# Handing the second quarter of a transposed residual to TensorE in two pairs of slices, with the third quarter's transposes between them

## The reference

```
def rmsnorm(x, g):
    return x * lax.rsqrt(mean(x * x, -1) + EPS) * g

def swiglu(x, w_gate, w_up, w_down):
    return (silu(x @ w_gate) * (x @ w_up)) @ w_down

for l in range(2):
    x = x + 0.5 * swiglu(rmsnorm(x, ffn1_norm[l]), ffn1_w_gate[l], ffn1_w_up[l], ffn1_w_down[l])
    h = rmsnorm(x, mix_norm[l])
    ...                                    # projections h @ w_in, attention, gated linear attention
    x = x + y @ w_out[l]
    x = x + 0.5 * swiglu(rmsnorm(x, ffn2_norm[l]), ffn2_w_gate[l], ffn2_w_up[l], ffn2_w_down[l])
return rmsnorm(x, final_norm)
```

## Time and profile before

| | |
|---|---|
| time, median of 3 runs | 2364.39 us (2362.51 to 2365.77) |
| profiled execution, its own time | 2362.39 us |
| span of the profile (first to last instruction) | 2360.7 us |
| TensorE (PE) busy | 2318.9 us, 98% |
| VectorE (DVE) busy | 1586.1 us, 67% |
| ScalarE (ACT) busy | 1139.8 us, 48% |
| granted TensorE clock, mean | 0.996 |

### The profile page before, as it was taken

How to read it: one execution, slowest core, us unless ns; L and a number is a source line. 1 busy time by engine, 2 the same in 40 slices (tenths; PEclk the granted TensorE clock), 3 DMA queues, 4 the chain that set the end, 5 groups by cost and what they waited for, 6 DMA issues and landing times.

```text
span 2360.7 us, 32903 instructions
## 1 busy us (share of the span) xinstructions
PE 2318.9 (98%) x13270; PEld 1954.5 (83%) x13270; DVE 1586.1 (67%) x2396; ACT 1139.8 (48%) x1668; POOL 24.9 (1%) x65
## 2 busy tenths in 40 slices
PE   6999999999999999999999999999999999999998
PEld 4887887888889887888888988888888888888887
DVE  4677434657575777667776679676676676776766
ACT  4222223446433255445445478554464446875444
POOL 0001000010000000000000000000000000000000
PEclk8999999999999999999999999999999999999999
DMA  7468322433522234655555643445545555434553
GB/s 306 179 233 323 140 90 94 148 116 143 195 90 72 72 108 171 228 191 178 181 194 192 233 160 143 161 178 184 191 179 196 184 203 214 148 144 173 189 196 125
DMA packets 59311, 403.75 MB, mean 171 GB/s; under 512 B 8269, under 2 KB 8677, under 8 KB 11672
## 3 DMA queue, kind: packets, MB, share of 16 engines
q1 hardware_dynamic: 52992, 384.33, 44.9%
q10 hardware_dynamic: 3840, 9.43, 1.1%
q0 software_dynamic: 2336, 7.96, 1.1%
HBM read 400.60 MB, written 2.67 MB: 171 GB/s over the span
## 4 chain that ended last, share of the span: by engine, by line
PE 93%; DVE 3%; DMA 2%; ACT 1%; issue 1%; SPq 0%; ACTq 0%; DVEq 0%
PE pair L527 88%; DMA ring<-in_stream 2%; PE pair L937 1%; PE pair L1083 1%; PE pair L886 1%; DVE ring_parts L2389 0%; DVE ring_parts L2379 0%; PE pair L625 0%; ACT xT L1566 0%; PE pair L1352 0%; PE pair L1367 0%; PE pair L925 0%; DVE rows L2511 0%; PE pair L1337 0%; DVE X L2517 0%
## 5 line engine op out<-in xcount | busy, mean ns | idle before, releaser
L527 PE MATMUL pair<-xT_parts,ring_high 128*128 128x512 f32 x2112 | 747.4, 395 | 3.8 <-DVE xT_parts L2294 1.2
L527 PE MATMUL pair<-xT_parts,ring_parts 128*128 128x256 f32 (+2 forms) x2448 | 693.1, 298 | 3.3 <-DVE xT_parts L2307 1.4
L2379 DVE TENSOR_TENSOR ring_parts<-ring,ring_high 128x2048 fp32r<-128x2048 f32 x194 | 444.1, 2292 | 137.8 <-ACT ring_high L1623 137.7
L527 PEld LDWEIGHTS pair<-xT_parts,ring_parts 128*128 128x128 f32 (+1 forms) x2448 | 460.4, 188 | 44.3 <-issue 8.7
L527 PEld LDWEIGHTS pair<-xT_parts,ring_high 128*128 128x128 f32 x2112 | 384.5, 188 | 81.2 <-issue 2.0
L1623 ACT ACTIVATE ring_high<-ring 128x2048 fp32r<-128x2048 f32 x197 | 375.5, 1910 | 68.1 <-DMA ring<-in_stream 68.0
L2389 DVE TENSOR_TENSOR ring_parts<-ring,mix_high 128x1024 fp32r<-128x1024 f32 x144 | 169.2, 1218 | 38.1 <-ACT mix_high L1636 38.1
L1674 ACT ACTIVATE arena<-pair 128x512 f32<-128x512 f32 x110 | 65.9, 599 | 260.1 <-PE pair L527 260.1
L1636 ACT ACTIVATE mix_high<-ring 128x1024 fp32r<-128x1024 f32 x144 | 143.4, 1048 | 92.3 <-DMA ring<-in_stream 89.0
L527 PE MATMUL pair<-ring_parts,xT_parts 128*128 128x512 f32 (+1 forms) x448 | 173.9, 388 | 0.6 <-DVE ring_parts L2389 0.6
L527 PE MATMUL pair<-ring_parts,g_high 128*128 128x512 f32 x440 | 172.2, 391 | 0.2 <-issue 0.2
(11 more groups left out here) (439 smaller groups left out, 3867.6 us busy)
## 6 DMA issues: line engine op xcount, KB each, us to landing
ring<-in_stream SPq DMA_DIRECT2D x338, 1024.0 KB, 4.8
xn<-in_mods SPq DMA_DIRECT2D x14, 1024.0 KB, 4.9
arena<-in_mods SPq DMA_DIRECT2D x14, 1024.0 KB, 4.9
gateB<-gate_rows POOLq DMA_DIRECT2D x4, 512.0 KB, 7.6
xn<-maximum_rows POOLq DMA_DIRECT2D x8, 256.0 KB, 3.6
arena<-in_bT ACTq DMA_DIRECT2D x1, 1536.0 KB, 9.5
bias_scratch<-bias_row POOLq DMA_DIRECT2D x1, 1536.0 KB, 8.7
X<-in_x ACTq DMA_DIRECT2D x1, 1024.0 KB, 11.9
```

The source lines that it names most:

```text
L527: m = pe.matmul(o, l, r, start=start, stop=stop)
L2379: dve.tensor_tensor(out=ring_r[:, slot].rearrange("p a b -> p (a b)"), in0=w, in1=high[:, slot, :], op=ALU.subtract).then_inc(low_ready, 1)
```

## The change

The second quarter (q = 1) goes over in two pairs of slices. ACT raises `x_whole` after its second slice too, DVE splits k = 0, 1 and k = 2, 3 in two steps (`split_raw(1, 0, 2)` ahead of `update(0, 1)`, `split_raw(1, 2, 4)` behind it, ahead of `first_vars`), so that `x_split` counts five steps at a boundary. TensorE begins the next stage after the first pair: up tile 0's part 0 is made for k = 0, 1, then turn 2 comes, then k = 2, 3, then turn 3. Turn 2 leaves the end of the stage before. In the mixer's `pre_group` features 0 and 1 are made together for k = 0, 1, then turn 2, then their k = 2, 3, then turn 3, then features 2 and 3. At the `double` boundary the row of roots moves from behind up tile 1 to a place inside up tile 2, after three slices of its first half. The order of `update(1, 1)`, `split_raw(2)` and `low_part(0)` on DVE stays.

```diff
 def raw_start():
-    c.split += 4
+    c.split += 5
     c.raw += 1
     for part in range(2):
         for f in range(2):
-            if f == 0:
-                pe.wait_ge(x_split, c.split - 2 + 2 * part)
+            if part and f == 0:
+                pe.wait_ge(x_split, c.split)
             if part == 0 and f:
                 pe.wait_ge(low_half, c.raw)
             else:
                 low_wait(f)
-            up_steps(f, f, [(half, range(CW * part, CW * part + CW)) for half in range(2)])
+            if part or f:
+                up_steps(f, f, [(half, range(CW * part, CW * part + CW)) for half in range(2)])
+            else:
+                for first in (0, 2):
+                    pe.wait_ge(x_split, c.split - 3 + first // 2)
+                    up_steps(f, f, [(half, range(first, first + 2)) for half in range(2)])
+                    if first == 0:
+                        turn_raw(raw[0], 2, raw[1])
             if part:
                 owed.append(read[(c.chunk + f) % SLOTS])
-                if f == int(double):
+                if f == 0 and not double:
                     root_row()
             elif f == 0:
                 turn_raw(raw[0], 3, raw[1])
...
+                    elif f == 2 and double:
+                        up_steps(j, f, [(0, range(3))])
+                        root_row()
+                        steps = [(0, range(3, KD)), (1, range(KD))]
...
-                        if raw_next and f == FT - 1 and (n, t_) != (0, 0):
+                        if raw_next and f == FT - 1 and (n, t_) in ((0, 1), (1, 0)):
                             turn_raw("down", 2 * n + t_ - 1, c.resid)
...
-                        if raw_next and part_ and i:
+                        if raw_next and part_ and i in (1, 2):
                             turn_raw("quad", i - 1, c.acc)
...
                 for part in range(2):
-                    if turned is not None:
+                    by_pair = 2 if first and part == 0 else 0
+                    if turned is not None and not by_pair:
                         pe.wait_ge(x_split, turned - (0 if part else 2 if span == S else CW))
-                    for b, at in fs:
...
-                        if first and part == 0 and b is fs[0][0]:
-                            first()
+                    for q in range(by_pair):
+                        pe.wait_ge(x_split, turned - 3 + q)
+                        for b, at in fs[0:2]:
+                            feature(b, at, range(2 * q, 2 * q + 2))
+                        first(2 + q)
+                    for b, at in fs[by_pair:]:
+                        feature(b, at, range(CW * part, CW * part + CW))
...
-                c.split += 4
+                c.split += 5
...
-                pre_group(range(4), turned=c.split, between=mix_root_row, first=lambda: turn_raw("down", 3, at))
+                pre_group(range(4), turned=c.split, between=mix_root_row, first=lambda q: turn_raw("down", q, at))
...
-                    ins.then_inc(x_whole, 1)
+                        if j == 3 or j == 1 and q == 1:
+                            ins.then_inc(x_whole, 1)
...
-                def split_raw(q):
+                def split_raw(q, first=0, end=4):
                     h, t_ = divmod(q, 2)
-                    ks, at = slice(4 * h, 4 * h + 4), S + t_ * P
+                    ks, at = slice(4 * h + first, 4 * h + end), S + t_ * P
...
                 split_raw(0)
+                split_raw(1, 0, 2)
                 update(0, 1)
+                split_raw(1, 2, 4)
                 first_vars(2)
-                split_raw(1)
                 update(1, 1)
                 split_raw(2)
                 low_part(0)
```

More of the change, by code:

```diff
@@ L1185, in pre_group, with feature @@
                 ts = [(pre_bank(), slice(t_ * P, (t_ + 1) * P)) for t_ in tokens]
+                def feature(b, at, ks):
+                    for k in ks:
+                        wl, wh = mix_weights(k, slice(at, at + rows), True, 1 if beside is None else 2)
+                        mm(b[0:rows, 0:span], wl, whole[:, k, 0:span], k == 0, False)
+                        mm(b[0:rows, 0:span], wh, rest[:, k, 0:span], False, False)
+                        mm(b[0:rows, 0:span], wh, whole[:, k, 0:span], False, k == KD - 1,
+                           pre_full if k == KD - 1 else None)
                 for part in range(2):
-                    if turned is not None:
+                    by_pair = 2 if first and part == 0 else 0
+                    if turned is not None and not by_pair:
                         pe.wait_ge(x_split, turned - (0 if part else 2 if span == S else CW))
-                    for b, at in fs:
[L1190 to L1195, removed]
-                        if first and part == 0 and b is fs[0][0]:
-                            first()
+                    for q in range(by_pair):
[5 more added lines that the diff above has]
+                        feature(b, at, range(CW * part, CW * part + CW))
                     for b, ts_ in ts:
```

## The result

The changed kernel takes 2372.61 us (median of 6 runs, 2371.21 to 2377.95), the kernel before 2364.39, so the medians differ by 8.2 us. The prediction was 2372.1 and the sum behind it 7.75.

A forecast was written before the change was run, and what follows sets the result against it. PE was taken as busy 98% of the span, with the chain at the quad running from turn 2 to up tile 1. Terms 2.92 + 1.43 + 2.9 + 0.5 = 7.75 us on 2364.4 gave 2372.1, range 2367.0 to 2379.0.

The forecast's parts named there:

- The way: From turn 2 to up tile 1, 4.15 us; at both quad boundaries up tile 1 comes 1.46 later, together +2.92.
- FFN down: Down boundary into layer 1's FFN: up tile 0 starts 0.91 us earlier, up tile 1 1.43 later.
- Mixers: Two mixer boundaries: start 0.91 us earlier, row of roots 0.25 later at each, +0.5 together.
- Double: Double boundary: up tile 2 0.55 us later, ACT's take of the row of roots 3.2, first down tile 2.9.
- the slack of 0.33: Double boundary: DVE's `low` was expected to end about 0.33 us before PE needs it for the first down tile.
- (a): Rival: the clock falls behind the five new waits, 1.56 us each, 7.8 in all, giving 2379.9; chance 0.12.
- the prediction's own signs of being wrong: Up tile 1 2.2 us behind turn 2, granted clock below 1.00 behind a wait, or first down tile without a wait.
- (b): Rival: not slower, the way from turn 2 to up tile 1 is hidden behind PE's 2.16 us, giving 2362.1; chance 0.15.
- (c): Rival: the later row of roots at the double boundary costs nothing, sum 5.4 us, giving 2369.8; chance 0.10.
- (d): Rival: no early hand-over of the first pair, three starts lose the 0.91 us, sum 10.5, giving 2374.9; chance 0.05.

The follow-up runs named there:

- The first experiment: The changed kernel with low_part(0) put ahead of split_raw(2) on DVE: 2364.76 us, ratio 1.0007 to the kernel before.
- the row of roots alone: The kernel before with only the double boundary's row of roots moved into up tile 2: 2368.42 us beside 2362.91, ratio 1.0019.

## Why the prediction was right

That the medians differ by 8.2 where 7.75 was forecast is closer than the runs can tell. What bears the account is that the terms come out one by one in the table of distances above.

**The way.** "Turn 2 1.46 later, and nothing on DVE was moved past quarter 2's split" was the step that decides. The way stayed 4.15 at the quads, and the segments lost 1.48 and 1.4 for 1.46. The new wait is 1.7 and not 2.0, since a wait is counted from turn 3's modelled end, 0.60 behind its start, and I had taken 0.35; the time is the same. The first experiment turned the two instructions round, and the loss went.

**FFN down.** Up tile 0 follows the first copy after 3.38 (1737.72 in the profile after to 1741.10) in place of 4.21, 0.83 earlier for 0.91; up tile 1 after 9.02 in place of 7.48, +1.54 for +1.43.

**Mixers.** 0.90 earlier for 0.91 at the start; the row of roots 10.94 behind the first copy (1302.53 after) in place of 10.65, +0.29 for +0.25, with the wait of 0.60 that was to be seen. The segments say 0.4; where the last tenth lies stays open.

**Double.** Against the copy of quarter 1, at 1111.39 after and 1111.28 before: up tile 2 +0.56 for 0.55, ACT's take of the row +3.28 for 3.2, the first down tile +2.97 for 2.9 (1136.75 - 1111.39 less 1133.67 - 1111.28). The 0.31 between the last two is the slack of 0.33. The segment lost 0.3 more than the tile; that is the one term a little too small.

**The rivals.** (a), the clock, came once in ten: of the five new waits in each of two executions of the changed kernel, one was followed by a fall, for 1.4 us more up to the mixer's first copy (192.96 against 191.54). That is the one of the prediction's own signs of being wrong that showed; it is not part of the sum, and the 8.5 without such a fall already is the whole difference of the medians. (b), not slower, named its own condition, another order on DVE; with that order, and the row of roots back, the time is that of before. (c) is out by the row of roots alone, whose first down tile comes 2.4 later. (d) is out: the start came 0.8 to 0.9 earlier.

## What to carry to other kernels

Before a step is moved later to let its neighbour start sooner, follow what it feeds: where that way already ends last, each microsecond of delay is lost, and the early start only turns into a wait further on. Look at what stands behind the moved step's successors in an in-order queue; turning round two steps there was worth 6.4 us by the medians (8.2 less 1.8). Compare two profiled executions from a landmark onwards, with the granted clock beside it, since a fall of the clock at a place that the change doesn't touch (3.4 us) can be larger than a term that you look for (2.8 for the row of roots).

## What the hardware did that was not expected

Whether the clock falls from 2.4 to 1.2 GHz behind a wait differs from one execution to the next. In the eleven profiled executions it fell behind the wait of 1.9 on L625 in nine, and behind the longer one of 2.2 on L642 in four. Of nineteen waits of 1.6 to 1.9 made by the change and its variants one was followed by a fall; of the four waits of 3.1 all were. So the length of the wait orders the new waits, but not the old ones. What PE does behind a wait differs too: on L625 and L642 it is 64 and 32 small products with `diag`, at the new waits a tile's wide products; no run varies that alone. The Trainium skill (TensorE: Matmul & The Clock Gate, Why this matters for your kernels) warns of idle gaps between bursts of matmuls. The waits of 3.1 agree with it; the wait on L625 is shorter than the gaps that it warns of, and the clock fell behind it all the same.

The falls at the two places are not independent. On L642 the clock fell in exactly the four executions in which the first fall began within 0.3 us of the end of the wait on L625 (at 410.70 behind a wait that ended at 410.42, in the kernel after). Where the first fall began 0.9 us or more behind it (at 411.70 behind 410.39, in the kernel before), or didn't come, the second stayed away. And without any long wait the clock fell five times in twenty-two behind a stretch of products on 16 and 64 partitions, for 2.9 to 3.5 us each, in kernels whose code there is the same. What decides between two executions of one kernel stayed open; the same page (Part 1: The HAM clock gate) says that the watch on the engine's activity runs free of the kernel, which would fit, but no run here shows the watch itself.
